# Interleaving the two column tiles of a split weight unit, so that TensorE reads its weights 8 bytes apart

## The reference

```python
D_MODEL, SEQ, D_FF = 2048, 256, 5632

def first_block(x, ...):                       # one layer
    h = rmsnorm(x, norm_mix)
    p = h @ w_in                               # 2048 x (512 + 3*768 + 2*768)
    y = concatenate([multiscale_pool_mixer(p...), hyena_mixer(p...), chunked_spatial_gating(p...)])
    x = x + y @ w_out
    h = rmsnorm(x, norm_ffn)
    up = dwconv3(h @ ffn_w_up, ffn_conv_w, ffn_conv_b)      # 2048 x 11264
    gate, val = split(up, 2)
    x = x + (silu(gate) * val) @ ffn_w_down                 # 5632 x 2048
    return rmsnorm(x, norm_final)

def second_block(x, mem, ...):                 # one layer
    h = rms_norm(x, norm_g)
    proj = h @ w_in                            # q, k, v, z of three mixers and three gates
    ya = chunked_band_attention(...) * silu(az)
    yb = rwkv7_time_mix(...) * silu(bz)
    yc = memory_cross_attention(cq, *split(rms_norm(mem) @ w_mem_kv)) * silu(cz)
    merged = sigmoid(ga) * (ya @ w_up_a) + sigmoid(gb) * (yb @ w_up_b) + sigmoid(gc) * (yc @ w_up_c)
    return x + merged @ w_o
```

## Time and profile before

| | |
|---|---|
| time, median of 2 runs (lowest to highest) | 2277.08 us (2273.8 to 2280.36) |
| the profiled execution: its time, its span | 2275.0 us, 2273.2 us |
| TensorE busy, matmuls / weight loads | 2253.7 us (99%) / 2218.8 us (98%), 22160 of each |
| VectorE busy | 1533.0 us (67%) |
| ScalarE busy | 1132.6 us (50%) |
| DMA | 401.44 MB, mean 177 GB/s |
| granted TensorE clock | 1.000 of full speed |

### The profile page before, as it was taken

The page is one execution under the profiler, slowest core; times in us unless marked ns, Lnnn a source line. Parts: engine busy times, 40 slices in busy tenths (PEclk is TensorE's granted clock), DMA queues, the critical chain, the costliest instruction groups (busy, mean ns, idle before and its releaser), DMA issues.

```text
span 2273.2 us, 54334 instructions
## 1 busy us (share of the span) xinstructions
PE 2253.7 (99%) x22160; PEld 2218.8 (98%) x22160; DVE 1533.0 (67%) x2125; ACT 1132.6 (50%) x1553; POOL 12.8 (1%) x27
## 2 busy tenths in 40 slices
PE   8999999999999999999999999999999999999999
PEld 7999999999999999999999999999999999999999
DVE  7658777666645666668887788888877555555554
ACT  6443445555434555544655566666656444444432
POOL 0000000000000000000000000000000000000000
PEclk9999999999999999999999999999999999999999
DMA  7453555555555555565545444444434455555554
GB/s 275 169 185 122 172 188 186 185 186 189 189 186 188 191 185 186 193 219 189 200 160 176 143 143 153 151 139 145 150 122 158 165 187 187 185 194 186 190 189 157
DMA packets 110534, 401.44 MB, mean 177 GB/s; under 512 B 12539, under 2 KB 12566, under 8 KB 110241
## 3 DMA queue, kind: packets, MB, share of 16 engines
q1 hardware_dynamic: 108288, 390.91, 51.5%
q0 software_dynamic: 2080, 8.06, 1.1%
HBM read 396.81 MB, written 2.10 MB: 175 GB/s over the span
## 4 chain that ended last, share of the span: by engine, by line
PE 96%; DVE 2%; ACT 1%; DMA 1%; issue 0%; SPq 0%; DVEq 0%; ACTq 0%
PE bank L461 95%; DVE w_lo L1651 1%; DMA raw<-in_units 1%; ACT m_b L1097 0%; ACT w_hi L1097 0%; DVE x L1700 0%; PE bank L901 0%; DVE prod L1697 0%; DVE acc L1697 0%; DVE scaled_in L1697 0%; PE bank L827 0%; SPq L1062 0%; ACT x L1180 0%; SPq L1067 0%; DVE fh L1704 0%
## 5 line engine op out<-in xcount | busy, mean ns | idle before, releaser
L1651 DVE TENSOR_TENSOR w_lo<-raw,w_hi 128x1024 fp32r<-128x1024 f32 x736 | 894.0, 1223 | 652.0 <-ACT w_hi L1097 647.0
L1097 ACT ACTIVATE w_hi<-raw 128x1024 fp32r<-128x1024 f32 x736 | 778.0, 1059 | 849.0 <-PE bank L461 840.2
L461 PE MATMUL bank<-h_hi,w_hi 128*128 128x256 f32 x4016 | 1135.3, 283 | 10.4 <-DVE h_lo L1700 10.4
L461 PE MATMUL bank<-h_lo,w_hi 128*128 128x256 f32 x4016 | 1122.3, 279 | 0.0
L461 PE MATMUL bank<-h_hi,w_lo 128*128 128x256 f32 x4016 | 1121.6, 279 | 0.0
L461 PEld LDWEIGHTS bank<-h_hi,w_hi 128*128 128x128 f32 x4016 | 755.8, 188 | 16.5 <-DVE h_lo L1700 10.4
L461 PEld LDWEIGHTS bank<-h_lo,w_hi 128*128 128x128 f32 x4016 | 756.1, 188 | 1.7
L461 PEld LDWEIGHTS bank<-h_hi,w_lo 128*128 128x128 f32 x4016 | 755.8, 188 | 0.0
L461 PE MATMUL bank<-m_hi,w_hi 128*128 128x256 f32 x704 | 196.7, 279 | 0.0
L461 PE MATMUL bank<-m_lo,w_hi 128*128 128x256 f32 x704 | 196.5, 279 | 0.0
L461 PE MATMUL bank<-m_hi,w_lo 128*128 128x256 f32 x704 | 196.5, 279 | 0.0
(11 more groups left out here) (435 smaller groups left out, 2636.8 us busy)
## 6 DMA issues: line engine op xcount, KB each, us to landing
raw<-in_units SPq DMA_DIRECT2D x736, 512.0 KB, 3.3
memx<-in_memT POOLq DMA_DIRECT2D x4, 512.0 KB, 8.7
out_y<-obuf SPq DMA_DIRECT2D x8, 256.0 KB, 4.3
x<-in_xT SPq DMA_DIRECT2D x3, 512.0 KB, 9.8
bias_t<-in_bias POOLq DMA_DIRECT2D x8, 192.0 KB, 3.3
dft<-in_dft POOLq DMA_DIRECT2D x1, 1024.0 KB, 11.0
decay<-in_decay POOLq DMA_DIRECT2D x1, 768.0 KB, 7.8
x<-in_xT SPq DMA_DIRECT2D x2, 256.0 KB, 5.5
```

Source lines behind the costliest of these rows:

```text
L461: return pe.matmul(out, lhsT, rhs, start=start, stop=stop, skip_group_check=True)
L1097: return act.activation(out, in_, ACT.Copy, scale=scale)
L1651: dve.tensor_tensor(w_lo[slot][:, :, :], raw[slot][:, :, :], w_hi[slot][:, :, :].bitcast(F32), ALU.subtract).then_inc(split_done, 1)
```

## The change

`w_hi` and `w_lo` change their layout inside a block: instead of column tile 0 (128 words) followed by column tile 1 (128 words), word `n` of tile 0 and word `n` of tile 1 now stand next to each other. ScalarE and VectorE read `raw` as before, and write (VectorE also reads `w_hi`) every second word: first the 128 even words of a block, then the 128 odd ones. TensorE's weight load of a tile reads 128 words that are 8 bytes apart. Sizes, transfers, semaphores, the order on every engine, the number of instructions on each (14540 in TensorE's program, 1286 in VectorE's, 901 in ScalarE's) and all other operands stay.

```diff
-        w_hi = [sb(f"w_hi{i}", [P, UK, UN], F32R) for i in range(RING)]
-        w_lo = [sb(f"w_lo{i}", [P, UK, UN], F32R) for i in range(RING)]
+        w_hi = [sb(f"w_hi{i}", [P, UK, UN // 2, 2], F32R) for i in range(RING)]
+        w_lo = [sb(f"w_lo{i}", [P, UK, UN // 2, 2], F32R) for i in range(RING)]
...
+        def in_blocks(t):
+            return t[:, :, :].rearrange("p k (e n) -> p k e n", e=2)
+
+        def by_turns(t):
+            return t[:, :, :, :].rearrange("p k n e -> p k e n")
...
# unit, and the same in part
-                        wh = w_hi[slot][:, kk, t * P:(t + 1) * P]
-                        wl = w_lo[slot][:, kk, t * P:(t + 1) * P]
+                        wh = w_hi[slot][:, kk, :, t]
+                        wl = w_lo[slot][:, kk, :, t]
...
# the units of ffn_w_down
-                        wh4 = w_hi[slot][:, :, :].rearrange("p k n -> p (k n)").rearrange("p (k n) -> p k n", k=2)
-                        wl4 = w_lo[slot][:, :, :].rearrange("p k n -> p (k n)").rearrange("p (k n) -> p k n", k=2)
...
-                                wh, wl = wh4[:, kk, t * P:(t + 1) * P], wl4[:, kk, t * P:(t + 1) * P]
+                                wh, wl = (w[slot][:, 2 * kk + t // 2, :, t % 2] for w in (w_hi, w_lo))
...
# ScalarE's split
-                copy(w_hi[slot][:, :, :], raw[slot][:, :, :]).then_inc(hi_done, 1)
+                copy(by_turns(w_hi[slot]), in_blocks(raw[slot])).then_inc(hi_done, 1)
...
# VectorE's split
-                dve.tensor_tensor(w_lo[slot][:, :, :], raw[slot][:, :, :], w_hi[slot][:, :, :].bitcast(F32),
+                dve.tensor_tensor(by_turns(w_lo[slot]), in_blocks(raw[slot]), by_turns(w_hi[slot]).bitcast(F32),
                                   ALU.subtract).then_inc(split_done, 1)
```

## The result

The changed kernel takes 2343.2 us (median of 2 runs, 2343.09 to 2343.28) against 2277.1 us before: 1.030 times as long, 95% interval 1.0284 to 1.0317. The prediction was 2337 us, range 2270 to 2385. The span of the profiled execution went from 2273.2 to 2341.3 us, + 68.1 us.

What follows compares the result with a forecast made beforehand. TensorE's unit matmul stream, 116.6 ns apart, was taken as the bound. 2275.0 us + 60 us for strided loads + 0 + 0 for the splits gave 2335 us, as a median of runs 2337 us, range 2270 to 2385.

Steps and rivals of the forecast that it cites:

- What bounds the kernel, and the count: TensorE has 96% of the chain; 17616 unit matmuls at 116.6 ns make 2054 of the 2273 us span.
- the 24 float32 loads: Contiguous 128-column float32 loads on TensorE, 111.7 ns each, taken as the most that a contiguous load needs.
- the z1 row: Twelve TensorE transposes loading a strided z1, 120.0 ns apart against 109.1 contiguous; taken as the strided load's need, 60 us.
- The z1 case: Likeliest case: strided unit loads set a distance of 119.2 to 122 ns, 2322 to 2372 us; chance 0.47.
- the hidden case: Rival: strided unit loads need no more than 116.6 ns and stay covered by the stream, 2277 us; chance 0.26.
- The two kinds of load look alike: Transposing z1 loads and plain fh loads, 194 and 193 ns long unpacked, so packed plain loads should resemble z1's.
- the fh row: Strided fh filter loads under 384 columns, 193 against 190 ns; read as a need of about 114.7 ns, costing nothing.
- ScalarE's split: 736 splits writing every second word, expected within 5% of 1059 ns; at worst twice as long, still hidden.
- In between: Rival: distance between 116.6 and 119.2 ns, a real cost under 2%, 2277 to 2322 us; chance 0.12.
- Adding: Rival: strided load and stream disturb each other, 10.9 ns on top of 116.6, 192 us, 2469 us; chance 0.08.
- VectorE as the bound: Rival: VectorE's split takes twice its length and VectorE binds, + 181 us, 2458 us; chance 0.05.
- The stride not there: Rival: compiled weight loads are contiguous after all and nothing moves; left in the small rest, 0.02.

Runs made afterwards that it cites:

- run 3: Kernel before with each unit matmul streaming 128 of its 256 columns, contiguous loads; 111.6 ns from matmul to matmul, 2255.2 us.
- run 5: Kernel before with 512-column unit matmuls and only every second block of a unit used; 233.1 ns apart, 2272.0 us, 0.9981 times.
- run 2: Kernel before with contiguous splits, but TensorE loads every second word of a block; 2342.3 us, 1.0294 times the kernel before.
- run 4: Interleaved layout with each unit matmul streaming 128 of its 256 columns; 119.0 ns from matmul to matmul, 2351.2 us.
- run 6: Interleaved layout with 512-column unit matmuls and only every second block of a unit used; 233.1 ns apart, 2274.9 us, 0.9997 times.
- run 11: Changed kernel with each unit matmul streaming 240 of its 256 columns; 2328.7 us.
- run 1: Changed kernel with TensorE loading 128 contiguous words of the interleaved buffers, splits still writing strided; 2276.5 us, 1.0014 times the kernel before.
- run 10: Kernel before with splits unchanged, but TensorE loads 128 words that are 16 bytes apart; 4316.8 us.
- run 9: Kernel before with splits unchanged, but TensorE loads 128 words that are 12 bytes apart; 3301.2 us.

## Why the prediction was right

- **What bounds the kernel, and the count.** Right. One distance times 17616 gives the result: 3.87 ns on average is the 68.1 us of the span. The window's own 120.9 - 116.6 = 4.3 ns would make 76 us; the average is lower since it covers the stages in which other matmuls stand between units, too. The start times of the same matmuls in both traces show it: a unit matmul costs 4.3 ns from 350 to 1030 us and after 1770 us of the kernel before, but 1.5 to 3.6 ns in the first 350 us and 3.6 from 1160 to 1620 us. Multiplying a window's distance by the whole count, as the prediction does, gives too much.
- **The stream sets the pace before, a load needs up to 111.7 ns.** Right, shown by runs 3 and 5: 111.6 ns beside 128 columns, 233.1 ns for 512 columns. But the prediction read its own row for it too simply. It says that the 24 float32 loads meet "a shorter stream"; that stream is float32 and not float32r. The kernel before has 11 such matmuls of 256 columns in its timeline:
```profile
206.43 2.54 PE L461 MATMUL bank<-gsq,con 128*128 128x256 f32 x11
```
  They start (2.54 - 0.38) / 10 = 216 ns apart (0.38 us is the length of one), so 128 float32 columns take an estimated 108 ns, hardly less than the 111.7 ns read there.
- **The strided load becomes the slower one, at 120.0 ns as in the z1 row.** Right in kind: run 2 puts the whole cost in the reads, run 4 shows the load alone over 116.6 ns, run 6 that it is free when covered. The size was taken as 3.4 ns and 60 us and came out at 3.87 ns and 68.1 us. The term 120.0 ns was mis-sized in two ways: the load beside 128 columns needs 119.0 ns, and beside 256 columns the distance is 120.9. Taking the larger of the two needs, 119.0, would have given 2.4 x 17616 = 42 us; the other 1.9 of the 4.3 ns come from load and stream together, which the prediction doesn't have, and their cause is open. That the z1 row gave a number so near was in part luck. Its twelve transposes stream 128 float32 columns, some 108 ns by the estimate above, so the row is a strided load beside a stream of about that length, and run 11, beside a float32r stream of some 109 ns, has the same 120.0. I hadn't seen that. Two more errors cancel in part: the distance in the window was taken too small, 3.4 ns for 4.3, and it was charged to all 17616 matmuls, which cost 3.87 on average.
- **How firmly it was held.** The z1 case had a chance of 0.47, and the range of 2270 to 2385 us holds the hidden case as well. That the time lies inside it says little; what bears the mechanism out is runs 1, 2, 4 and 6.
- **"The two kinds of load look alike".** Half right. Loads of z1 are 209 ns long, and I expected near 209 for the unit loads; they are 197. The start-to-start distance carried over, the length didn't. By the fh row the prediction turned 3 ns of length (193 against 190 ns) into 3 ns of need, for its hidden case. That was a wrong reading: a unit load's length grew by 9 ns and its need by 7.4. The fh load, of 64 rows and covered by 384 columns, could not show its need.
- **ScalarE's split.** I expected it within 5%; it got 10% longer (1162 against 1059 ns), so that expectation was wrong. It is hidden as predicted: run 1, with all strided writes, costs 0.14%.
- **VectorE's split.** Unchanged, as predicted: 1225 ns.
- **The rivals.** Hidden: refuted by runs 2 and 4. In between, under 2.6 ns: refuted by the 4.3 ns, though the 119.0 ns of run 4 alone, 2.4 over the stream, would have ended there. Adding, 10.9 ns on top: refuted by the 120.9 ns, where it has 127.5. VectorE as the bound: refuted by its 1225 ns. The stride not there: refuted by the longer loads and run 2.

## What to carry to other kernels

A stream of load and matmul pairs has two times in it, and the hidden one matters as soon as an edit lengthens it: divide a window by its count for the distance, find a place where the other one binds for its need, and compare the two before touching a layout. Here a stationary operand at 8 bytes instead of 4 raised the load's need from 111.6 to 119.0 ns, just past the 116.6 ns of a 256-column float32r stream, and cost 3%; at 16 bytes the kernel took 1.9 times as long (run 10), and under 512 columns a load at 8 bytes costs nothing. For a small excess, don't count on the larger of the two times: with the strided load the distance was above both, by 1.9 ns beside a stream of 116.6 ns and by 1 ns beside shorter ones. With the contiguous load, 5 ns under the stream, it was the stream's own, half of the 233.1 ns of 512 columns.

## What else the runs showed of the hardware

- One strided load among contiguous ones costs more than its share: 6.7 ns for one in three, against 12.9 for all three.
- A float32r stream of 256 or 512 columns runs at 0.456 ns a column (116.6 and 233.1 ns), a float32 stream of 256 at 0.84 (216 ns).
- With 128 columns per matmul TensorE ran at half its pace for stretches. In run 3, windows of all engines from 60 to 100 and from 1680 to 1720 us:
```profile
60.00:100.00 40.00, 40.00 (x153) 33.94 (x153) 19.41 (x26) 8.20 (x10) 1.64 (x3) 1.00 0.24 81
1680.00:1720.00 40.00, 40.00 (x199) 38.94 (x199) 17.06 (x24) 12.64 (x19) 0.00 (x0) 0.50 0.28 93
```
The second has a granted clock of 0.50, its lower level of 1.2 GHz, and 199 matmuls in 40 us. It fell there at 1668.5 us and rose at 1719.7; before it fell TensorE had been busy for 39.2 of the 40 us up to 1640 and idle for at most 0.9 us at a time from there. The first window is as slow, 153 matmuls where the changed kernel has 300, though its clock column says 1.00. The column has nothing to go by there: the trace's record of the clock starts at 112 us in run 3 and at 113 us in run 4, and at 12 to 15 us in all the others, and in each of them unit matmuls keep a slower pace up to that moment (213 ns from start to start in runs 3 and 4) and the one of the rest of the run from it on. This is why the total times of runs 3 and 4 say little. Matmul by matmul, run 4 is 41 us behind the changed kernel where that one is at 100 us, and wins 33 back in the rest, for 2351.2 us in all; run 3 (2255.2 us) is 41 us behind the kernel before at the same place. Why the slow stretch lasts so long with 128 columns is open.
- At the lower clock the stride costs nothing. Start to start a unit matmul takes 213 ns there in the kernel before, in the changed kernel, with 128, 192 and 240 columns and with words 12 bytes apart (run 9); only words 16 bytes apart (run 10) show, with 240 ns. These are the first microseconds of every run, before the record starts, so that the clock there was the lower one is inferred from the same 213 ns in run 3 where the record has 0.50. Two matmuls in a row of run 4, then of the changed kernel, from the timeline of TensorE:
```profile
11.23 0.41 PE L467 MATMUL bank<-h_hi,w_hi 128*128 128x128 f32 x1
11.44 0.41 PE L467 MATMUL bank<-h_lo,w_hi 128*128 128x128 f32 x1
```
```profile
11.03 0.41 PE L467 MATMUL bank<-h_lo,w_hi 128*128 128x256 f32 x1
11.24 0.41 PE L467 MATMUL bank<-h_hi,w_lo 128*128 128x256 f32 x1
```
  So the 7.4 ns of the stride are there at the full clock alone. That the distance doesn't move from 128 to 240 columns also speaks for what run 3 assumes, that at 128 columns the load sets it.
